# Query and output products of two cross attentions: from plain float32 operands to split operands in three products

## The reference, cut to what matters

```python
def cross_attn(h, wq, q_norm_g, mk, mv, wo):
    bsz, seqlen, _ = h.shape
    q = rmsnorm((h @ wq).reshape(bsz, seqlen, MEM_HEADS, MEM_HEAD_DIM), q_norm_g)
    s = jnp.einsum('blhd,bmhd->bhlm', q, mk.astype(q.dtype)).astype(jnp.float32) * (MEM_HEAD_DIM ** -0.5)
    p = jax.nn.softmax(s, axis=-1)
    o = jnp.einsum('bhlm,bmhd->blhd', p.astype(h.dtype), mv.astype(h.dtype))
    return o.reshape(bsz, seqlen, MEM_DIM) @ wo
```

## Time and profile before

| | |
|---|---|
| median of three runs | 1919.51 us (1917.16 to 1920.94) |
| the profiled execution's own time | 1917.64 us |
| its span in the trace | 1915.8 us |
| mean granted TensorE clock | 0.987 |
| PE busy | 1845.5 us, 96% of the span |
| DVE busy | 810.2 us, 42% |
| ACT busy | 454.4 us, 24% |
| POOL busy | 144.6 us, 8% |
| HBM | 84 GB/s over the span |

### The profile page before, as it was taken

How to read it: one execution, slowest core, us unless ns; L and a number is a source line. 1 busy time by engine, 2 the same in 40 slices (tenths; PEclk the granted TensorE clock), 3 DMA queues, 4 the chain that set the end, 5 groups by cost and what they waited for, 6 DMA issues and landing times.

```text
span 1915.8 us, 26533 instructions
## 1 busy us (share of the span) xinstructions
PE 1845.5 (96%) x11334; PEld 1564.6 (82%) x11334; DVE 810.2 (42%) x1287; ACT 454.4 (24%) x720; POOL 144.6 (8%) x149
## 2 busy tenths in 40 slices
PE   7999988998999999999989997999999999999998
PEld 5566566556799999999979996655559999999997
DVE  4599835225544423444332305422344443244422
ACT  4011232014421111122221134410433221111111
POOL 3021100000000000000042332100000000000000
PEclk9999989999999999999999998999999999999999
DMA  7222420232321122211202252402322211222120
GB/s 238 94 94 76 116 76 6 77 132 100 121 77 59 61 89 88 69 71 61 96 22 89 88 67 92 169 24 103 139 67 88 69 63 62 102 82 71 45 96 34
DMA packets 32036, 161.50 MB, mean 84 GB/s; under 512 B 8584, under 2 KB 9224, under 8 KB 18016
## 3 DMA queue, kind: packets, MB, share of 16 engines
q1 hardware_dynamic: 24032, 121.97, 19.6%
q0 software_dynamic: 7936, 38.60, 5.6%
HBM read 149.87 MB, written 10.42 MB: 84 GB/s over the span
## 4 chain that ended last, share of the span: by engine, by line
PE 93%; DVE 4%; ACT 1%; issue 1%; DMA 0%; SPq 0%; POOL 0%; ACTq 0%; DVEq 0%
PE G L670 88%; PE S L670 2%; PE Q L670 2%; DVE front L1608 1%; PE Q L1184 1%; PE Q L1034 0%; ACT rstd L1251 0%; DVE stats L2103 0%; ACT work L1251 0%; ACT front L1251 0%; DMA par<-in_par 0%; DVE front L2118 0%; DVE stats L1880 0%; DVE rstd L1639 0%; ACT mkT L1251 0%
## 5 line engine op out<-in xcount | busy, mean ns | idle before, releaser
L670 PE MATMUL G<-h_split,w_split 128*128 128x320 f32 x5184 | 763.3, 309 | 0.0
L670 PEld LDWEIGHTS G<-h_split,w_split 128*128 128x128 f32 x5184 | 760.4, 188 | 0.2 <-issue 0.2
L670 PE MATMUL G<-front,ring 128*128 128x128 f32 (+2 forms) x1792 | 485.5, 432 | 5.2 <-issue 1.7
L670 PEld LDWEIGHTS G<-front,ring 128*128 128x128 f32 x1792 | 278.7, 192 | 211.9 <-issue 205.5
L1251 ACT ACTIVATE w_split<-ring 128x1024 fp32r<-128x1024 f32 (+2 forms) x172 | 164.9, 960 | 753.0 <-PE G L670 753.0
L670 PE MATMUL G<-g_split,w_split 128*128 128x320 f32 x2112 | 310.4, 309 | 0.0
L670 PEld LDWEIGHTS G<-g_split,w_split 128*128 128x128 f32 x2112 | 309.9, 188 | 0.0
L1646 DVE TENSOR_TENSOR w_split<-ring,w_split 128x1024 fp32r<-128x1024 f32 (+2 forms) x152 | 164.4, 1083 | 140.9 <-ACT w_split L1251 140.6
L1979 DVE TENSOR_TENSOR work<-work,G 128x640 f32<-128x640 f32 x44 | 36.1, 821 | 203.8 <-PE G L670 203.8
L1709 DVE SCALAR_TENSOR_TENSOR front<-front,par 128x512 f32<-128x512 f32 x240 | 113.6, 548 | 0.1
L1970 DVE TENSOR_TENSOR work<-G,rstd 128x640 f32<-128x640 f32 x44 | 36.3, 825 | 129.8 <-PE G L670 116.5
(11 more groups left out here) (225 smaller groups left out, 1117.1 us busy)
## 6 DMA issues: line engine op xcount, KB each, us to landing
ring<-in_w_up0a SPq DMA_DIRECT2D x11, 1024.0 KB, 4.9
ring<-in_w_up0b SPq DMA_DIRECT2D x11, 1024.0 KB, 4.9
ring<-in_w_up1a SPq DMA_DIRECT2D x11, 1024.0 KB, 4.9
ring<-in_w_up1b SPq DMA_DIRECT2D x11, 1024.0 KB, 4.8
front<-in_mem_k POOLq DMA_DIRECT2D x8, 1024.0 KB, 7.6
front<-in_mem_v POOLq DMA_DIRECT2D x8, 1024.0 KB, 9.6
ring<-in_w_down0a SPq DMA_DIRECT2D x8, 704.0 KB, 4.0
ring<-in_w_down0b SPq DMA_DIRECT2D x8, 704.0 KB, 4.1
```

The source lines that it names most:

```text
L670: return nc.tensor.matmul(out, lhsT, rhs, start=start, stop=stop, **kw)
```

## The change

Both products of both cross attentions go from `project` to `split_product`. So that their operands exist in two parts:

- The query input `hq` is now a pair of rows per feature block. ACT writes the high row (`high_row`), DVE the low row (`low_row`), behind each tile of the mixer's output product. The plain scaling of line 2033 is gone.
- The weights of `q` are split into a buffer `wq`, those of `wo` into `wo_split`. The two pieces of the first `q` chunk are split behind row 6 of the mixer's output, the two of the second behind query tiles 0 and 1. The first two pieces of `wo` are split after the attention's loop, ahead of `run_results`; the other six behind the tiles 0 to 5 of `wo`, one each.
- `results` and `run_results` write the attention's result twice: a copy to the high part, a wait of DVE for that copy (`own`), and a subtraction of it from what is still in PSUM into the low part.
- The ring's places of `q` and `wo` chunks are free when both pieces are split, not when the tiles are finished.
- Caches and operands have other places in `front`, and the residual reads `wo` tiles from the middle of the PSUM buffer (`GF`).

The diff, without the new places of buffers in `front` and some renamed arguments:

```diff
@@ -135,8 +135,10 @@
 def _cross_ffn(l):
-    _chunks("q" + l, 2, WCH, _pairs("q" + l))
-    _chunks("wo" + l, 4, 4 * 256, _pairs("wo" + l))
+    for name, count, width in (("q" + l, 2, WCH), ("wo" + l, 4, 4 * 256)):
+        PIECE0[name] = PIECE0["_"]
+        PIECE0["_"] += 2 * count
+        _chunks(name, count, width, lambda i: -(PIECE0[name] + 2 * i + 2))
@@ -232,6 +234,9 @@
         tmp = work[:, 2:4, :]
+        with nc.sbuf_tensor("wo_split", [P, 2, LAYERS, MH * MT], F32R) as wo_split:
+            pass
...
@@ -440,13 +449,20 @@
-            up, buf = name[0] != "d", ws if name[0] in "ud" else ws1
-            w = ring[:, (CHUNK[name] + u) % RING, 0:WCH if up else HALF * P]\
-                .rearrange("p (k n) -> p k n", k=KD if up else HALF)
+            up = name[0] != "d"
+            rows = 4 if name[0] == "w" else KD if up else HALF
+            w = ring[:, (CHUNK[name] + u) % RING, 0:rows * (256 if up else P)].rearrange("p (k n) -> p k n", k=rows)
             src = w[:, :, s * P:(s + 1) * P] if up else w[:, s * KS:HALF if s else KS]
             KT = src.shape[1]
-            parts = [buf[:, s, part, 0:KT * P].rearrange("p (k n) -> p k n", k=KT) for part in range(2)]
+            parts = [split_weights(name, s, part)[:, 0:KT * P].rearrange("p (k n) -> p k n", k=KT) for part in range(2)]
             return src, parts[0], parts[1]
+        def split_weights(name, s, part):
+            if name[0] == "w":
+                return wo_split[:, s, int(name[2]), part * 512:(part + 1) * 512]
+            buf = wq if name[0] == "q" else ws if name[0] in "ud" else ws1
+            return buf[:, s, part, :]
...
@@ -696,7 +712,7 @@
-            def split_product(n, slot, p, KT, rhs, weights=ws, before=None, normed=None, start=0, stop=True):
+            def split_product(n, slot, p, KT, rhs, weights="up", before=None, normed=None, start=0, stop=True):
@@ -707,7 +723,7 @@
                     for wpart, xpart in ((0, 0), (0, 1), (1, 0)):
-                        w = weights[:, slot, wpart, k * P:(k + 1) * P]
+                        w = split_weights(weights, slot, wpart)[:, k * P:(k + 1) * P]
@@ -998,7 +1014,11 @@
-                projections(f"q{l}", 4, KD, hq, norm=f"cross{l}", after=lambda n: n and query_stat(n - 1))
+                for n in range(4):
+                    split_product(TILE0[f"q{l}"] + n, n % 2, PIECE0[f"q{l}"] + n, KD, hq, f"q{l}",
+                                  normed=None if n else APPLIED[f"cross{l}"] - KD + 1)
+                    if n:
+                        query_stat(n - 1)
...
@@ -1076,7 +1096,8 @@
                 read_wait(pe, TILE0[f"xt{l}"] + 1)
-                projections(f"wo{l}", 8, 4, rows(xo))
+                for n in range(8):
+                    split_product(TILE0[f"wo{l}"] + n, n % 2, PIECE0[f"wo{l}"] + n, 4, xo, f"wo{l}")
...
@@ -1309,6 +1330,9 @@
+            def high_row(out, j, gain):
+                A(out[:, 0, j, :], x[:, j, :], ACT.Copy, scale=pr(gain, j)).then_inc(h_hi, 1)
@@ -1455,7 +1479,9 @@
                 act.wait_ge(outs, 16 * (ODD_OUTS if l else SCAN_OUTS))
-                head_norms(lambda j: xq[:, j, :], TILE0[f"q{l}"], 4, 1.0 / P, eps=5)
+                t0 = TILE0[f"q{l}"]
+                head_norms(lambda j: xq[:, j, :], t0, 4, 1.0 / P, eps=5, out=GF,
+                           after=lambda j: j < 2 and high_part(f"q{l}", 1, j, tile_done, t0 + j + 1))
@@ -1481,9 +1507,13 @@
                         turned(it - 2)
+                for s in range(2):
+                    high_part(f"wo{l}", 0, s, tile_done, TILE0[f"xo{l}"] + 8)
                 def ffn_rows(j):
-                    A(hs[:, 0, j, :], x[:, j, :], ACT.Copy, scale=pr(f"ffn{l}", j)).then_inc(h_hi, 1)
+                    high_row(hs, j, f"ffn{l}")
+                    if j < 6:
+                        high_part(f"wo{l}", j // 2 + 1, j % 2, tile_done, TILE0[f"wo{l}"] + j + 1)
@@ -1525,7 +1555,13 @@
-            residual_squares("evout")
+            def query_rows(l, name, j):
+                high_row(hq, j, f"cross{l}")
+                if j == 6:
+                    high_part(f"q{l}", 0, 0, tile_done, TILE0[name] + 1)
+                    high_part(f"q{l}", 0, 1, run_added, 4)
+            residual_squares("evout", lambda j: query_rows(0, "evout", j))
@@ -1585,7 +1621,8 @@
                     fox_turned(it - 2)
-            residual_squares("odout")
+            act.wait_ge(outs, 16 * ODD_OUTS)
+            residual_squares("odout", lambda j: query_rows(1, "odout", j))
@@ -1612,11 +1649,11 @@
-            def add_residual(name, after=None, total=None):
+            def add_residual(name, after=None, total=None, out=G):
                 for j in range(KD):
...
                     tile_wait(dve, n)
-                    v.tensor_tensor(x[:, j, :], x[:, j, :], G[n % 2][:, 0:T], ALU.add)\
+                    v.tensor_tensor(x[:, j, :], x[:, j, :], out[n % 2][:, 0:T], ALU.add)\
@@ -1638,6 +1675,13 @@
                 nadd[0] += 1
+            def low_row(out, j, gain, rows):
+                dve.wait_ge(h_hi, rows + j + 1)
+                v.scalar_tensor_tensor(out=out[:, 1, j, :], in0=x[:, j, :], scalar=pr(gain, j),
+                                       in1=out[:, 0, j, :].bitcast(F32), op0=ALU.mult, op1=ALU.subtract)\
+                    .then_inc(applied, 1)
@@ -1900,8 +1944,10 @@
                         qt, hh = it // 2, 2 * (it % 2)
-                        ins = v.tensor_copy(xo[:, hh:hh + 2, qt * P:(qt + 1) * P],
-                                            o[:, 0:2 * P].rearrange("p (s q) -> p s q", s=2))
+                        hi, lo = (xo[:, part, hh:hh + 2, qt * P:(qt + 1) * P] for part in range(2))
+                        o = o[:, 0:2 * P].rearrange("p (s q) -> p s q", s=2)
+                        own(v.tensor_copy(hi, o))
+                        ins = v.tensor_tensor(lo, o, hi.bitcast(F32), ALU.subtract)
@@ -1913,13 +1959,20 @@
                     tile_wait(dve, n)
-                    for sl in range(2):
-                        at = SEQ + (2 * (it - 8) + sl) * 2 * STEP
-                        for odd in range(2):
-                            src = G[n % 2][:, (2 * sl + odd) * P:(2 * sl + odd + 1) * P]\
-                                .rearrange("p (e g c) -> p e g c", e=2, g=2)[:, :, :, odd * STEP:(odd + 1) * STEP]
-                            ins = v.tensor_copy(xo[:, odd::2, at:at + 2 * STEP]
-                                                .rearrange("p g (e t) -> p e g t", e=2), src)
+                    for part in range(2):
+                        for sl in range(2):
+                            at = SEQ + (2 * (it - 8) + sl) * 2 * STEP
+                            for odd in range(2):
+                                src = G[n % 2][:, (2 * sl + odd) * P:(2 * sl + odd + 1) * P]\
+                                    .rearrange("p (e g c) -> p e g c", e=2, g=2)[:, :, :, odd * STEP:(odd + 1) * STEP]
+                                hi, lo = (xo[:, i, odd::2, at:at + 2 * STEP].rearrange("p g (e t) -> p e g t", e=2)
+                                          for i in range(2))
+                                if part == 0:
+                                    ins = v.tensor_copy(hi, src)
+                                else:
+                                    ins = v.tensor_tensor(lo, src, hi.bitcast(F32), ALU.subtract)
+                        if part == 0:
+                            own(ins)
@@ -1931,6 +1984,8 @@
                 add_eps(0)
+                for s in range(2):
+                    low_part(f"q{l}", 1, s)
@@ -1946,18 +2001,19 @@
                         results(it - 3)
+                for s in range(2):
+                    low_part(f"wo{l}", 0, s)
                 for it in range(8, NX):
...
                 def ffn_rows(j):
-                    dve.wait_ge(h_hi, KD * l + j + 1)
-                    v.scalar_tensor_tensor(out=hs[:, 1, j, :], in0=x[:, j, :], scalar=pr(f"ffn{l}", j),
-                                           in1=hs[:, 0, j, :].bitcast(F32), op0=ALU.mult, op1=ALU.subtract)\
-                        .then_inc(applied, 1)
+                    low_row(hs, j, f"ffn{l}", 2 * KD * l + KD)
+                    if j < 6:
+                        low_part(f"wo{l}", j // 2 + 1, j % 2)
                     if j == 5:
...
-                add_residual(f"wo{l}", ffn_rows)
+                add_residual(f"wo{l}", ffn_rows, out=GF)
@@ -2029,8 +2085,10 @@
             def query_row(l, name, j):
-                read_wait(dve, TILE0[name] + j)
-                v.tensor_scalar(hq(j), x[:, j, :], pr(f"cross{l}", j), None, ALU.mult).then_inc(applied, 1)
+                low_row(hq, j, f"cross{l}", 2 * KD * l)
+                if j == 6:
+                    for s in range(2):
+                        low_part(f"q{l}", 0, s)
...
                 query_row(0, "evout", j)
```

(32 more changed lines are left out.)

## The result

The changed kernel took 1906.12 us as the median of five runs (1899.95 to 1909.78), the kernel before 1918.78 us (1917.16 to 1920.94). The ratio is 0.993 with a 95% interval of 0.991 to 0.9951: faster by 0.7%, some 13 us. The forecast of 1901 was too low by 5 us; the time lies within the range of 1896 to 1908.

The account below looks back on a forecast made before the run. PE was taken to bound the kernel. Per layer -12.8 + 0.3 + 2.2 + 0.1 + 1.3 = -8.9 us, twice -17.8, gave 1899.8 us for the profiled execution, 1901.7 on the median, stated as 1901; range 1896 to 1908.

Parts of the forecast that it names:

- both products: Query and output product of each cross attention: split matmuls take 6.4 us less each, -12.8 us per layer.
- the rival of products that are not shorter: Both products: fp32r operands in new places are read at another pace, no gain, 1927 us; chance 0.02.
- The stretch ahead of the output product: Between attention and output product: DVE's weight pieces, copies and subtractions take 3.7 us for 1.52, +2.2 us per layer.
- The prompt iterations: Attention's prompt iterations: a wait and subtraction on DVE after each result, +0.3 us per layer, ends 0 and 2.25.
- The carried delay: Prompt iterations: 0.45 us per result, less idle time before five maxima, leaves 0.01, 0.46, 0.91, 0.92 and 0.17 us.
- The output product's cover: Output product: each weight piece is ready 0.04 us early behind its tile; 0.1 us taken per layer, ends 0 and 4.1.
- The rival of a limiting weight piece: Output product: half to the whole weight piece delays each of 12 tiles, 4.1 to 8.3 us, 1906 to 1910; chance 0.14.
- The clock: Around the output product's start: one fall to 1.2 GHz per layer after the longer PE idle time, +1.3 us, ends 0 and 1.7.
- the sum of 1899.8: Whole kernel: the profiled execution's 1917.64 us less 17.8 us for both layers gives 1899.8 us.
- the three stages of the table: First cross attention: query product -6.4, from there to output product +2.5, output product with first SwiGLU tile -6.3 (clock +1.3).
- the same term's bad end: Clock around the output product's start: a fall costs at most 1.7 us per layer.
- Slower rival: Output product: the clock stays at 1.2 GHz throughout, 28.2 us more per layer, 1955 us; chance 0.03.

Follow-up runs that it names:

- version with the early pieces: Changed kernel with the first two `wo` weight pieces split while DVE waits for the request products, not behind them: 1898.44 us, ratio 0.9891.
- the kernel before with its reductions: Kernel before, nothing split, plus three unread DVE reductions of 512 columns ahead of the small copies: 1925.65 us, ratio 1.0041.
- the three filled versions: Unread matmuls ahead of the output product: three in the changed kernel (1900.45 us); three (1897.13) or one (1896.27) with weight pieces moved earlier.

## Why the prediction was right, and where it was off

- **What bounds, and both products.** PE's path, as said. The query product gave -6.45 us per layer against -6.4, with its splitting hidden; the version with the query products alone confirms it. The output product gave -6.46 us (41.89 to 35.43) once its waits were gone. The pace of 0.147 us per matmul held in the new places: the rival of products that are not shorter is out.
- **The stretch ahead of the output product.** +2.1 us against +2.2, instruction by instruction as listed. The version with the early pieces shows that 1.2 us of it was on the path only by the place of two pieces in DVE's order.
- **The prompt iterations.** Mis-sized: +0.65 us per layer, where 0.3 was taken between 0 and 2.25. The carried delay was right in kind. It failed at its last step, where the idle time of 1.20 us was to bring the delay down from 0.92 to 0.17 us. That idle time is a wait for PE, which had become later too, and 0.78 us of it stayed.
- **The output product's cover.** Mis-sized: the piece that was to be 0.04 us early is 0.1 us late on every second tile, 0.4 us per layer instead of 0.1. The rival of a limiting weight piece has the right mechanism, at 0.7 us for both layers where 4.1 to 8.3 were set.
- **The clock.** The step was right in place, cause and price of one fall (1.4 to 1.5 us in the changed kernel, 1.7 in the kernel before with its reductions). It was wrong in expecting one fall per layer: whether one comes differs from run to run, and in one trace between the layers. The profiled run had no fall at all and came out at 1899.95 us, next to the sum of 1899.8, which contained 2.6 us for it. Three things made up for these 2.6 us: the three stages of the table together gained 0.4 us per layer less than their forecast without the clock, the rest of the kernel was 0.75 us longer, and the time outside the span was 2.95 us instead of 1.84. That agreement is luck, and it hides how far the forecast was from the median.
- **The failed part** is the same term's bad end. The prediction took at most 1.7 us per layer. Three of the changed kernel's five traces have falls, one of them a fall of 2.6 us, and filling the idle time gains 5.1 us in the median, 4.4 of them in the span, more than the 3.4 us that the bound allows. Runs with a clock of 0.987 take 1899.4 to 1900 us, with 0.984 some 1903.6, with 0.981 they take 1907.4 to 1909.3. A mean clock lower by 0.006 (0.981 for 0.987) means 2 x 0.006 x 1904 = 23 us more at 1.2 GHz, where the traces of the changed kernel show at most 3.4 + 6.8 = 10.2 us in the two output products.
- **What stays open:** where the rest of these 23 us lies in the runs of 1907 us and more. None of them was traced. That the new idle time makes such runs common is shown by the three filled versions, which have none in 12 runs. How it leads to so much more time at the lower level is not, and the scan and the second mixer's attention, where the traces of one and the same kernel differ as well, are not ruled out as places.
- **Slower rival.** The clock came back after one or two low stretches in every trace. Had it stayed down through the product, the piece of 35.80 us would be above 60 us.

## What to carry to other kernels

When a product gets shorter, look at what must be ready ahead of it. Small preparatory instructions of another engine that stood in a short wait can cost more than their own time, because TensorE's clock can fall behind the longer idle time. Here 2.1 us of DVE work per layer took a third of the output product's gain, it took half together with the other two small losses (0.65 and 0.4 us), and the clock took most of the rest. Put such work into waits that exist already, and where none is left, try a matmul whose result nobody reads in the gap, sized to end before the operands are ready. One profiled run of such a kernel says little about its median: compare the granted clock of all runs first.

## What the runs showed of the hardware

- Idle times of PE of 0.76 us (the kernel before, and one matmul left 0.82) had no fall behind them in the output products of their traces; 1.68 us had falls in both layers of one trace and in none of another; 2.88 us in neither, one or both layers of the changed kernel's five traces, and in both layers with the output products alone; 2.54 us had falls in both layers of the trace of the kernel before with its three reductions. So the same idle time, in the same program, sometimes costs nothing and sometimes 1.4 to 2.6 us. What decides it isn't shown here.
- A low stretch in these places measured 3.4 us at 1.2 GHz, or 6.8 us. One of 3.4 us lay wholly in the output product, beginning about 0.9 us after PE had started again, and cost 1.5 us and not 1.7. Why it cost less isn't shown.
- Traces of one and the same kernel also differ in the clock of the scan (0.72 to 0.86 over 24 us), and by up to 3.2 us in the time of that stage.
- Three matmuls whose result nobody reads, 2.6 us of PE work per layer, make this kernel 5 us faster, 0.7 us of it outside the span.
